# The merge of a hybrid trunk: from plain tiled products to one level of Strassen's scheme

## The reference, cut to what matters

```
o   = o_f + flip(o_b)
o   = o * rsqrt(mean(o*o, per head) + eps) * norm_g * silu(z_a)
y_a = o   @ w_pa          # 2048 x 1024 by 1024 x 1024
y_b = o_y @ w_pb          # o_y: the Hyena branch's output
m   = sigmoid(g_a) * y_a + sigmoid(g_b) * y_b
out = rmsnorm(x + gt * (m @ w_out), final_g)
```

## Time and profile before

| | |
|---|---|
| median of 3 runs | 4343.41 us (4341.93 to 4346.67) |
| the profiled execution's own time | 4344.41 us |
| its span, first to last instruction | 4342.6 us |
| TensorE busy | 4163.5 us, 96% of the span |
| VectorE, ScalarE, GpSimd busy | 2469.1, 1195.1, 1746.6 us |
| mean granted TensorE clock | 0.983 of full speed |
| DRAM traffic | 405.01 MB read, 217.53 MB written |

### The profile page before, as it was taken

How to read it: one execution, slowest core, us unless ns; L and a number is a source line. 1 busy time by engine, 2 the same in 40 slices (tenths; PEclk the granted TensorE clock), 3 DMA queues, 4 the chain that set the end, 5 groups by cost and what they waited for, 6 DMA issues and landing times. The chain is left out here.

```text
span 4342.6 us, 73281 instructions
## 1 busy us (share of the span) xinstructions
PE 4163.5 (96%) x29395; PEld 2525.9 (58%) x29395; DVE 2469.1 (57%) x3548; ACT 1195.1 (28%) x2531; POOL 1746.6 (40%) x1486
## 2 busy tenths in 40 slices
PE   5999999999999999999979999999999997999998
PEld 3455544444444444444448888856565656767766
DVE  6667754533467868886536666567676763222221
ACT  4112111111211111111125555565555551000000
POOL 1322333333333333433359989654444452112111
PEclk8999999999999999999989999999999998999999
DMA  8233222232333333334357798477767687224220
GB/s 294 65 91 100 91 78 81 86 107 100 116 126 109 106 109 103 96 121 131 121 159 211 218 285 223 138 218 214 222 197 223 217 254 272 78 77 144 88 78 29
DMA packets 480925, 627.12 MB, mean 144 GB/s; under 512 B 120784, under 2 KB 379800, under 8 KB 469980
## 3 DMA queue, kind: packets, MB, share of 16 engines
q1 hardware_dynamic: 431594, 484.22, 36.7%
q0 software_dynamic: 28560, 113.25, 8.1%
q10 hardware_dynamic: 20450, 25.17, 1.7%
HBM read 405.01 MB, written 217.53 MB: 143 GB/s over the span
## 5 line engine op out<-in xcount | busy, mean ns | idle before, releaser
L1534 PE MATMUL proj_b<-shared_S,proj_tw 128*128 128x512 f32 x1920 | 848.1, 593 | 0.0
L1534 PEld LDWEIGHTS proj_b<-shared_S,proj_tw 128*128 128x128 f32 x1920 | 360.4, 190 | 432.6 <-issue 431.7
L1534 PE MATMUL proj_b<-shared_A,shared_wt 128*128 128x512 f32 x1280 | 577.8, 594 | 9.5 <-PEq L159 8.9
L863 POOL TENSOR_TENSOR proj_tw<-shared_wt 128x512 f32<-128x512 f32 x80 | 115.4, 1442 | 880.5 <-PE proj_b L1534 813.4
L1534 PEld LDWEIGHTS proj_b<-shared_A,shared_wt 128*128 128x128 f32 x1280 | 243.9, 191 | 314.3 <-issue 313.9
L1534 PE MATMUL proj_b<-shared_A,proj_tw 128*128 128x512 f32 x640 | 289.5, 595 | 2.8 <-DVE proj_u L1176 2.8
L1534 PE MATMUL proj_b<-shared_S,shared_wt 128*128 128x512 f32 x640 | 290.1, 596 | 0.0
L1079 ACT ACTIVATE proj_v<-proj_b 128x512 f32<-128x512 f32 x80 | 47.8, 597 | 662.4 <-PE proj_b L1534 662.4
L1898 DVE SCALAR_TENSOR_TENSOR delta_la<-delta_kkq,bridge_region,delta_wm 128x256 f32<-128x256 f32 (+1 forms) x288 | 121.5, 463 | 170.5 <-PE delta_kkq L1998 170.3
L1534 PEld LDWEIGHTS proj_b<-shared_A,proj_tw 128*128 128x128 f32 x640 | 122.1, 191 | 157.5 <-issue 150.4
L1171 DVE TENSOR_TENSOR proj_u<-proj_b,proj_u 128x512 f32<-128x512 f32 x80 | 55.2, 690 | 274.9 <-PE proj_b L1534 274.8
(11 more groups left out here) (361 smaller groups left out, 8642.6 us busy)
## 6 DMA issues: line engine op xcount, KB each, us to landing
shared_wt<-in_w_in_dram POOLq DMA_DIRECT2D x80, 1024.0 KB, 5.9
scratch_bounce_f<-tail_first SPq DMA_DIRECT2D x128, 256.0 KB, 4.4
bridge_region<-scratch_bounce_f SPq DMA_DIRECT2D x32, 1024.0 KB, 7.4
scratch_bounce_i<-fft_yi SPq DMA_DIRECT2D x64, 512.0 KB, 3.5
fft_second<-scratch_bounce_i SPq DMA_DIRECT2D x32, 1024.0 KB, 8.4
scratch_hy<-shared_hA SPq DMA_DIRECT2D x48, 512.0 KB, 2.6
delta_ring<-scratch_NV SPq DMA_DIRECT2D x96, 256.0 KB, 4.1
delta_ring<-scratch_KQ SPq DMA_DIRECT2D x88, 256.0 KB, 4.3
```

What stands on the lines that cost most here:

```text
L863: pool.tensor_tensor(T3, w[:, hi, second], w[:, lo, second], ALU.subtract).then_inc(combined, 1)
L1534: last = pe.matmul(bank[:, :], weights[:, k, :], aa[operand][:, k, :], start=(k == 0), stop=(k == KH - 1))
```

## The change

The merge is written anew. It now works in four windows of 512 tokens with twelve units each, 48 in all: four units for `w_pa` (kind 0), four for `w_pb` (kind 1), four for `w_out` (kind 2), all unrolled. A unit makes the four quarters C11, C12, C21, C22 (each 128 x 256) of its part of the product, by seven products P1 to P7 of four matmuls with 256 columns. Even units use banks 0 to 3, odd ones banks 4 to 7 (first half of each bank; the second halves take the transposes of heads). ScalarE copies P1; VectorE forms the sums U2, U3, U4 and the quarters out of PSUM, gates them, and adds.

Each pair of units loads its own columns of the weights (two DMAs of 1 MB from SP), and GpSimd makes four combinations of them (128 x 1024). The combinations of the data operands are made on VectorE: of the attention operand and of `yT` once a window (128 x 1024 each, four of them), of `m` for each unit of kind 1 (128 x 256). Four token tiles are normed in Hyena's last step, with their transposes in new bank uses "W"; the later twelve within units 3 to 10 of the first three windows (`SUM_AT`: sums at r = 3, 4, 7, 8, means and scales one unit later, transposes and weighing two units later). GpSimd no longer gates or adds results.

The core of the diff:

```diff
+            if t == STEPS:
+                use(*[("W", 0, n) for n in range(4)])
             if t and t % 2 == 0:
                 use(*[("Z", t // 2 - 1, n) for n in range(8)])
+            if t == STEPS:
+                use(*[("W", 0, n) for n in range(4, 8)])
...
+                    if t == STEPS - 1:                     # Hyena, SP, behind the reads of bounce_i
+                        ready(sp, "T", t, N2 - 1)
+                        load_quarters(sp, T, "zaT", tail_ops(first), 0, L["za_in"])
+                        for i in range(2, 4):
+                            load_heads(sp, T, tail_o(L, i), i, L["o_in"][i])
+                        ready(sp, "M", t, N2 - 1)
+                        load_gates(sp, T, tail_gates(L, 0), 0, L["g_in"])
...
                 def merge_weights():
                     last = STEPS - 1
                     ready(pool, "A", last, N2 - 1)
+                    for i in range(2):
+                        load_heads(pool, T, tail_o(L, i), i, L["o_in"][i])
                     ready(pool, "Z", NCB - 2, 7)
+                    load_weights(pool, T, tail_raw(L, 0), 0, L["w_in0"])
...
                 def merge_operands():                      # GpSimd
+                    pair_heads((0, 1))
+                    pool.wait_ge(L["w_in0"], 32)
+                    for n in range(4):
...
+                        combine_weights(pool, tail_raw(L, 0), tail_mixed(L), n, L["combined"])
+                    pair_heads((2, 3))
...
                     if t == STEPS:                         # Hyena, VectorE
-                        first_norms()
+                        first_norms((0, 1))
                     for c in range(4):
                         if t:
                             outputs(t - 1, c)
...
+                    if t == STEPS:
+                        first_norms((2, 3))
+                        first_weights((0, 1))
                     if t and t % 2 == 0:
                         empty_out(t // 2 - 1)
+                    if t == STEPS:
+                        first_weights((2, 3))
...
+                for U in range(NUNIT):                     # merge, GpSimd
+                    tile = prepared(U, 0)
+                    if tile is not None:
+                        pair_heads(tile)
+                    g = U // 2 + 1
+                    if U % 2 and g < NGROUP:
+                        weights_landed(pool, g)
+                        multiplied_by(pool, U, "P7")
+                        combine_weights(pool, raw[g % 2], mixed, 0, combined)
+                        combined_to(pool, g, 1)
+                        combine_weights(pool, raw[g % 2], mixed, 1, combined)
+                        multiplied_by(pool, U, "P5")
+                        combine_weights(pool, raw[g % 2], mixed, 2, combined)
+                        combined_to(pool, g, 2)
+                        multiplied_by(pool, U, "P4")
+                        combine_weights(pool, raw[g % 2], mixed, 3, combined)
...
+                def quarter(U, name, first, second, into):     # merge, VectorE
+                    dve.tensor_tensor(into, first, second, ALU.add).then_inc(dve_summed, 1)
...
+                    if kind == 0:
+                        dve.tensor_tensor(block, into, gate, ALU.mult).then_inc(placed, 1)
+                        return
...
+                    if kind == 1:
+                        dve.tensor_tensor(into, into, gate, ALU.mult).then_inc(gated, 1)
+                        dve.wait_ge(gated, done + 1)
+                        dve.tensor_tensor(block, into, block, ALU.add).then_inc(placed, 1)
+                        return
...
+                def last_quarter(U):
+                    multiplied_by(dve, U, "P3")
...
+                    quarter(U, "C12", V, u4, V)
+                    row_mixes(U, (3,))
...
+                for U in range(NUNIT):
+                    w, r = divmod(U, UNITS_A_WINDOW)
+                    last_quarter(U - 1)
+                    mean(prepared(U, 1))
+                    if r == 11 and w + 1 < WINDOWS:
+                        for n in (2, 3):
+                            mix(ops[0], n, a_mixed, 4 * (w + 1))
+                    X, Y, Z, V = sets[U % 2]
+                    multiplied_by(dve, U, "P6")
+                    copied(dve, U)
+                    dve.tensor_tensor(u2, Y, u1, ALU.add).then_inc(dve_summed, 1)
...
+                    multiplied_by(dve, U, "P7")
+                    dve.tensor_tensor(u3, Z, u2, ALU.add).then_inc(dve_summed, 1)
+                    scale(prepared(U, 1))
+                    multiplied_by(dve, U, "P5")
+                    dve.tensor_tensor(u4, V, u2, ALU.add).then_inc(dve_summed, 1)
+                    quarter(U, "C22", V, u3, Y)
+                    weigh(prepared(U, 2))
+                    multiplied_by(dve, U, "P2")
+                    quarter(U, "C11", X, u1, X)
...
+                    if r == 10 and w + 1 < WINDOWS:
+                        for n in (0, 1):
+                            mix(ops[0], n, a_mixed, 4 * (w + 1))
+                    final_scale(U - 1)
+                    multiplied_by(dve, U, "P4")
+                    quarter(U, "C21", Z, u3, Z)
+                    row_mixes(U, (0, 1, 2))
...
+                for U in range(NUNIT):                     # merge, TensorE
+                    emptied(pe, U - 2, "C11")
...
+                    product(U, "P1", "A11", wt[:, lo, 0, :], X)
+                    combined_to(pe, g, 2)
+                    product(U, "P6", "S2", T2, Y)
+                    product(U, "P7", "S3", T3, Z)
+                    turn(U)
+                    emptied(pe, U - 2, "C12")
+                    combined_to(pe, g, 3)
+                    product(U, "P5", "S1", T1, V)
+                    copied(pe, U)
+                    product(U, "P2", "A12", wt[:, hi, 0, :], X)
+                    summed(pe, U, "U3")
+                    combined_to(pe, g, 4)
+                    product(U, "P4", "A22", T4, Z)
+                    summed(pe, U, "C22")
+                    product(U, "P3", "S4", wt[:, hi, 1, :], V)
```

More of the change, by code:

```diff
@@ new lines, in first_norms @@
+                    if 0 in tiles:
+                        dve.wait_ge(L["small"], 32)
+                    for i in tiles:
+                        dve.wait_ge(L["squared"], i + 1)
+                        dve.tensor_reduce(ms[:, i, :], heads(tail_o(L, i)[:, 1, :]), AX, ALU.add).then_inc(L["reduced"], 1)
+                        dve.wait_ge(L["reduced"], i + 1)
+                        dve.scalar_tensor_tensor(out=ms[:, i, :], in0=ms[:, i, :], scalar=1.0 / P, in1=epsq[:, NCTX + i, :], op0=ALU.mult, op1=ALU.add).then_inc(L["meaned"], 1)
@@ L2843, in _, with store, weights @@
-                windows(sp, window)
-                sp.wait_ge(stored, 16 * (NG + 1))
+                def store(U):
+                    w, _, _, j = place(U)
+                    for n, a in enumerate((j, 2 + j)):
+                        sp.wait_ge(normed, final_count(U) + n + 1)
+                        first = w * 2 * MQ + a * P
+                        sp.dma_start(T["out"][0][first:first + P, :], x[:, a, :]).then_inc(stored, 16)
+                def weights(g):
+                    load_weights(sp, T, raw[g % 2], g, w_in[g % 2])
@@ new lines, in mean @@
+                def mean(tile):
+                    if tile is None:
+                        return
+                    dve.wait_ge(squared, tile - 3)
+                    dve.tensor_reduce(ms[:, tile % 4, :], heads(head_tile(tile)[:, 1, :]), AX, ALU.add).then_inc(reduced, 1)
+                    dve.wait_ge(reduced, tile - 3)
+                    dve.scalar_tensor_tensor(out=ms[:, tile % 4, :], in0=ms[:, tile % 4, :], scalar=1.0 / P, in1=epsq[:, NCTX + tile, :], op0=ALU.mult, op1=ALU.add).then_inc(meaned, 1)
@@ L3047, in _, with product @@
-                windows(pe, window)
+                def product(U, name, operand, weights, bank):
+                    w, kind, G, j = place(U)
+                    if kind == 0 and operand in MIXES:
+                        pe.wait_ge(a_mixed, 4 * w + MIXES.index(operand) + 1)
+                    if kind == 1:
+                        pe.wait_ge(y_in, 64 * (w + 1))
+                        if operand in MIXES:
+                            pe.wait_ge(y_mixed, 4 * w + MIXES.index(operand) + 1)
+                    if kind == 2:
+                        pe.wait_ge(m_mixed, 16 * (w + 1))
+                    mine = slice(j * P, (j + 1) * P)
+                    for k in range(KH):
+                        data = ops[kind][operand][:, k, :]
+                        if kind < 2:
+                            last = pe.matmul(bank, weights[:, k, mine], data, start=(k == 0), stop=(k == KH - 1))
+                        else:
+                            last = pe.matmul(bank, data[:, mine], weights[:, k, :], start=(k == 0), stop=(k == KH - 1))
+                    last.then_inc(multiplied, 1)
@@ new lines, in taken, with turn @@
+                def taken(U, b):
```

(13 more changed lines are left out.)

659 lines of the change are left out of this document (355 added, 304 removed).

## The result

| | before | after |
|---|---|---|
| median, same chip | 4343.45 us (4341.93 to 4346.67, 4 runs) | 4294.84 us (4293.48 to 4303.42, 4 runs) |
| profiled execution | 4344.41 us | 4295.96 us |
| its span | 4342.6 us | 4294.1 us |
| first product of the merge starts | 3640.60 | 3644.47 |
| last product starts | 4328.81 | 4279.88 |

The ratio is 0.9891, with a 95% interval of 0.9874 to 0.9908: 49 us less, faster. The forecast was 4301 us.

What follows compares the result with a forecast made beforehand. The merge was taken as bound by TensorE's matmuls. First product at 3645.2, 590.4 of matmuls and turns, 53.5 of stalls and slow clock, and 10.6 at the end gave a 4299.7 us span, forecast 4301 us, range 4264 to 4328.

Steps and rivals of the forecast that it cites:

- entry of kind 2: Units 8, 20, 32, 44: TensorE waits for the window's last row mix, 6.0 us each, 24 us in all.
- unit 11: Windows 0 to 2: P4 waits for U3 behind operand mixes that meet GpSimd's combinations, 4 us each, 12 us.
- turn of unit 6: The turn of transposes in unit 6 waits for C12 of unit 5, three times, 2.2 us in all.
- The matmuls: Merge on TensorE: 2688 instructions at 0.2157 us plus twelve turns, 590.4 us against 689.1, 98.7 us less before new stalls.
- VectorE's instructions that write PSUM: Merge: 256-column VectorE instructions writing PSUM were taken at 0.42 us, between bounds of 0.42 and 0.69 us.
- rival B: Merge: VectorE sets the pace if its instructions take 0.69 us; 4341 us, no gain; chance 0.07.
- The block by GpSimd: Merge: a VectorE mix with both inputs in SBUF stands for up to a whole GpSimd instruction, 2.35 us.
- Rival A: Merge: GpSimd's work costs VectorE next to nothing, so stalls total 21.2 us; 4268 us; chance 0.22.
- The clock: TensorE's clock falls behind seven stalls of 4 to 6 us, costing 1.9 us each, 13.3 us in all.
- The start: First product of the merge starts at 3645.2 us, 4.6 us later than before, behind VectorE's weighing and copies.
- The end: After the merge's last product: C12, squares, roots, scale and a half-size store, 10.6 us against 12.9 before.
- Rival C: Merge: weights loaded again each window set the pace below 171 GB/s; 4392 us at 160 GB/s; chance 0.04.

Runs made afterwards that it cites:

- e4_eight: The kernel after with P1 of each unit multiplied twice, so eight products a unit; 4370.09 us, ratio 1.0061 to the kernel before.
- e1_hold: The kernel after with GpSimd's third and fourth combination in units 7, 19, 31, 43 held until all row mixes are done; 4273.03 us.
- e6_zact: The kernel after with ScalarE copying all of the last eight Z banks of the Hyena stage and VectorE none; 4294.24 us.
- e9_noload: The kernel after with weights from the sixth group on not loaded again, stale ones used instead; 4294.83 us.
- e2_own: The kernel after with each product of a window's first kind 2 unit waiting only for its own operand, not all sixteen mixes; 4277.40 us.
- e8_short: The kernel after with P4 run over only one of its four slices of the contracted dimension; 4260.98 us.
- e7_all: The kernel after with GpSimd held in units 7 and 11, products waiting for their own operands, and last Z copies all on ScalarE; 4252.62 us.

## Why the prediction was right, step by step

The span in the terms of the sum, forecast and measured in the profiled execution:

| term | forecast, us | measured, us |
|---|---|---|
| P1 of the first unit starts | 3645.2 | 3644.5 |
| 2688 instructions and 12 turns | 590.4 | 592.7 (what is left of the stretch) |
| entry of kind 2, four times | 24 | 27.8 |
| unit 11, three times | 12 | 3.2 |
| turn of unit 6, three times | 2.2 | 0 |
| slow clock behind the waits | 13.3 | 10.7 |
| slow clock and wait at the start | 2 | 2.7 |
| from the last product's end | 10.6 | 12.5 |
| span | 4299.7 | 4294.1 |

- **The matmuls.** Right. The pace is that of the earlier trace rows, 1.73 us from product to product, and e4_eight shows the price of a product directly. An ordinary unit takes 12.09 us, where 12.08 was forecast, so next to nothing of the 98.7 us was lost inside the units. Of the 2.3 us in the table's second row, the turns have 0.5; the rest is small gaps.
- **VectorE's instructions that write PSUM.** They had no row; 0.42 was taken between 0.42 and 0.69. They take 0.415 to 0.433 us (L3111) and 0.432 to 0.433 us (L3121, L3131). VectorE is busy for 454.5 us in the merge, 114 us a window, where the sum had 118. With that rival B, which needed 0.69, is out; its idea shows only where the unit is cut to 10.8 us.
- **The block by GpSimd.** Right, and the core of the case. One row, 2.17 against 1.27 us, was the evidence; here the mixes take 2.44 and 2.56 us beside GpSimd, and in e1_hold 0.42 at the same place. The Trainium skill (SBUF — State Buffer, § SBUF: two separate sides) says that the pair of ports is held for a whole instruction. The trace agrees: a mix ends 0.28 us after GpSimd does, however long it has stood, and at half its rate it would have taken at most 0.84 us (an estimate, twice 0.42; the prediction's 0.7 was loosely put). Rival A (4268 us) is thereby refuted as a statement on this kernel. In e1_hold the collision is avoided, and the waits are the 2.8 to 3.5 us that A had (3.2), without the slow clock that A put behind them; it comes to 4273.
- **The entry of kind 2.** 27.8 us against 24. The mechanism held, one party was missing from the walk: I walked GpSimd's four combinations and forgot that the head pair of unit 8 (L3009) follows the fourth without a pause and blocks one mix more. The waits are 7.64, 7.16 and 7.64 us in the three windows with that pair, and 5.32 in the last, which has none; there the third mix takes 0.41 us and not 2.56. I had put 6.0 for each.
- **Unit 11.** 1.06 us each, where I had 4. The mis-sized term is when VectorE comes free: C12 of unit 10 ends 4.5 us after the unit's start, not 5.5, so the first of the two operand mixes slips in ahead of GpSimd's first combination (from 5.4) and only the second pays. A microsecond of VectorE's queue decided over a whole GpSimd instruction. The turn of unit 6 is of the same kind: C12 of unit 5 ends 5.1 us after the start and not 5.9, and the turn comes 0.15 us late and not 0.7 (in the table this stands in the second row).
- **The clock.** The lower level came behind the four long waits and the start, as forecast, and cost 2.5 to 3.0 us each (1.9 forecast). Behind the three short ones of unit 11 it did not come. So the total, 10.7 against 13.3 us, looks nearer than its parts: seven times 1.9 was put where it was four times 2.7.
- **The start.** 3644.5 against 3645.2. GpSimd's second pair runs from 3622.9, the queue of weighing, copy, weighing on VectorE sets the end as walked: 3643.3, where I had 3642.7. But the agreement within 0.7 us is partly luck. The barrier and the first matmul took 1.2 us behind that queue and not 2.5, and Hyena's last store of `bounce_i` was issued at 3597.75 us, 2.1 us later than before, which no term had; so the outputs ended at 3625.8 and not 3621.2. What I had not seen is the bound right behind the queue, the transposes (e6_zact).
- **The end.** 12.5 against 10.6 us: the step that was missing is VectorE's order. Its last scales of unit 46 stand ahead of C21 of the last unit, so C21 began at 4282.41 us, though P4's result was ready at about 4280.1, and C12 at 4283.68, 1.9 us after its own product could be used (about 4281.8). That is the whole difference; the last store took 4.6 us to the end of the span against my 4.2, and squares, roots and scale 0.3 us less than I had.

```profile
4281.21 1.29 DVE L3162 SCALAR_TENSOR_TENSOR tail_u<-tail_u,tail_dlt,mrg_rows 128x1024 f32<-128x1024 f32 x1
4282.41 0.43 DVE L3111 TENSOR_TENSOR mrg_b<-mrg_b,tail_fan 128x256 f32<-128x256 f32 x1
...
4283.68 0.42 DVE L3111 TENSOR_TENSOR mrg_b<-mrg_b,tail_fan 128x256 f32<-128x256 f32 x1
```

- **The loads.** Rival C (4392 us) is out: weights land 6.3 to 7.4 us after their issue, GpSimd never waits for them, and e9_noload is no faster without them. C's limit of 171 GB/s was no test of it: the merge runs at 170 GB/s on average because it asks for no more, and some stretches of it reach 353.

So the time was met within 6 us, with the mechanism right and some luck in the number, by a sum in which the waits of unit 11 were 8.8 us too large and the entry of kind 2 with the tail 5.7 us too small. The range of 4264 to 4328 held it.

## What to carry to other kernels

Before an instruction of VectorE with both inputs in SBUF is put on a path, look at what GpSimd runs at that microsecond, with everything that follows it without a pause: a chain of short instructions pays one long GpSimd instruction for each of its links. It may be enough to hold back the engine that isn't urgent; here two lines that make GpSimd wait won 22 us on top of the 49 of the change. And a wait written for a whole phase ("all sixteen mixes") costs most where the phase's last piece is late; let each consumer wait for its own piece.

## What the runs showed of the hardware

- VectorE and GpSimd on SBUF alone: a VectorE mix of 0.42 us takes 2.44 to 2.60 us when it starts just after a GpSimd instruction of 2.35 us does, and ends 0.28 us after it. Longer ones end later: one of 128x512 (0.69 us alone) ended 0.54 us after GpSimd (L2487 at 3623.40 us, 2.38 us long), one of 128x1024 (1.22 us alone) 1.08 us after. In all three that is 0.14 to 0.15 us less than their own time, so at most that much of an instruction's work is done while it stands. The block goes both ways: GpSimd's 2.35 us became 3.21 us beside a 128x1024 one of VectorE. VectorE instructions with one input in PSUM take 0.42 to 0.43 us through all of this: L3111, L3121 and L3131 never exceed 433 ns.
- TensorE's clock: the granted clock fell from 1.00 to 0.50 behind waits of 4.0 us and more (4.0 to 4.3 in e2_own and e8_short, 5.3 to 8.2 elsewhere) and did not behind those of 1.06, 1.87, and 2.8 to 3.5 us (e1_hold). That is no rule of length: in the kernel before it did behind one of 2.60 us, and at the merge's first product, where TensorE had done only some transposes, behind 2.90 us (e7_all) and not behind 3.18 us (e6_zact). What decides stayed open. The slow clock cost 2.5 to 3.0 us more behind the four waits of after (5.3 to 7.6 us) and 1.5 to 2.9 behind those of e6_zact. In e1_hold the waits were 15.9 us shorter and the clock gave another 10.7: where the clock is saved too, shortening a wait wins more than the wait.
